# Last projection behind the last gate, running sums begun early, and the right half of the gates as products of split operands

## The reference

```python
h = layer_norm(DEEPNORM_ALPHA * x + mix, ln1_g, ln1_b)
logits = h @ router_w + router_b               # 32 experts, the top 4 for each token
# for each chosen expert e, over the rows sent to it:
gate, up = split(h @ w_gate_up[e] + b_gate_up[e])
y = ((clip(up) + 1) * min(gate, 7) * sigmoid(1.702 * gate)) @ w_down[e] + b_down[e]
ffn = sum over the 4 chosen experts of softmax weight * y
ple = sigmoid(h @ ple_w_gate) * (p @ ple_w_proj)
x = layer_norm(DEEPNORM_ALPHA * h + ffn + ple, ln2_g, ln2_b)
# second block: RMS norm, projections, attention and a recurrence, FFN, RMS norm
```

## Time and profile before

| | |
|---|---|
| median of 3 runs | 2106.93 us (2105.21 to 2108.22) |
| the profiled execution's own time | 2108.97 us |
| its span, first to last instruction | 2107.1 us |
| PE busy | 2073.0 us, 98% of the span |
| DVE, ACT, POOL busy | 1548.6, 1136.7, 237.1 us |
| granted clock of TensorE, mean | 0.993 |

### The profile page before, as it was taken

One profiled execution on the slowest core, in us unless ns is written; L12 is line 12 of the kernel. 1 busy time (PEld: TensorE's weight loads), 2 busy tenths in 40 slices (PEclk: granted clock), 3 DMA queues, 4 the chain that ended last, 5 costly groups with the idle time before them and its releaser, 6 DMA issues.

```text
span 2107.1 us, 26298 instructions
## 1 busy us (share of the span) xinstructions
PE 2073.0 (98%) x9292; PEld 1629.9 (77%) x9292; DVE 1548.6 (73%) x1431; ACT 1136.7 (54%) x1054; POOL 237.1 (11%) x239
## 2 busy tenths in 40 slices
PE   8999999999999999999999999989999999999998
PEld 4864478888888888888888888868886678888887
DVE  6986289999999999999999999974773344333333
ACT  3132177777777777777777777753124523122222
POOL 0006211111111111111111111100000000000000
PEclk9999999999999999999999999999999999999999
DMA  5233499999999999999999999932221213222321
GB/s 223 90 140 124 176 361 383 379 387 377 384 378 384 380 382 379 384 378 386 377 384 378 386 378 384 365 134 80 71 90 61 80 40 110 93 89 98 120 80 40
DMA packets 79062, 522.31 MB, mean 248 GB/s; under 512 B 10352, under 2 KB 10880, under 8 KB 22048
## 3 DMA queue, kind: packets, MB, share of 16 engines
q1 hardware_dynamic: 66496, 483.88, 59.1%
q0 software_dynamic: 9056, 30.62, 5.7%
q10 hardware_dynamic: 3456, 7.06, 1.0%
HBM read 500.92 MB, written 18.60 MB: 247 GB/s over the span
## 4 chain that ended last, share of the span: by engine, by line
PE 94%; DVE 4%; ACT 1%; issue 1%; DMA 0%; DVEq 0%; SPq 0%; ACTq 0%
PE bank L1088 26%; PE bank L1090 26%; PE bank L1089 26%; PE bank L1080 5%; PE bank L1268 1%; PE bank L1406 1%; PE bank L1097 1%; PE bank L1466 1%; PE bank L1225 1%; PE bank L1485 1%; PE bank L1260 1%; PE bank L1126 1%; PE bank L1501 1%; PE bank L1475 1%; DMA ring<-in_wd 0%
## 5 line engine op out<-in xcount | busy, mean ns | idle before, releaser
L1808 DVE TENSOR_TENSOR ring_r<-ring,room_r 128x2048 fp32r<-128x2048 f32 x384 | 875.2, 2294 | 78.6 <-ACT room_r L745 72.6
L745 ACT ACTIVATE room_r<-ring 128x2048 fp32r<-128x2048 f32 x384 | 736.2, 1918 | 175.0 <-PE bank L1090 168.2
L1089 PE MATMUL bank<-ring_r,room_r 128*128 128x512 f32 x1744 | 680.3, 390 | 0.0
L1088 PE MATMUL bank<-room_r 128*128 128x512 f32 x1576 | 624.1, 396 | 3.6 <-DVE room_r L1851 1.9
L1090 PE MATMUL bank<-room_r 128*128 128x512 f32 x1568 | 612.8, 391 | 0.0
L1089 PEld LDWEIGHTS bank<-ring_r,room_r 128*128 128x128 f32 x1744 | 328.5, 188 | 67.3 <-issue 1.7
L1088 PEld LDWEIGHTS bank<-room_r 128*128 128x128 f32 x1576 | 296.9, 188 | 65.7 <-DVE ring_r L1808 4.2
L1090 PEld LDWEIGHTS bank<-room_r 128*128 128x128 f32 x1568 | 295.1, 188 | 62.9
L1088 PE MATMUL bank<-room_r,ring_r 128*128 128x512 f32 x520 | 203.5, 391 | 1.7 <-DVE room_r L2154 0.9
L1090 PE MATMUL bank<-room_r,ring_r 128*128 128x512 f32 x512 | 199.3, 389 | 0.0
L1089 PE MATMUL bank<-ring_r 128*128 128x512 f32 x384 | 149.5, 389 | 0.0
(11 more groups left out here) (289 smaller groups left out, 2137.4 us busy)
## 6 DMA issues: line engine op xcount, KB each, us to landing
ring<-in_wmoe SPq DMA_DIRECT2D x384, 1024.0 KB, 12.0
ring<-in_wf SPq DMA_DIRECT2D x33, 1024.0 KB, 4.8
ring<-in_wd SPq DMA_DIRECT2D x7, 2048.0 KB, 9.4
ring<-in_wp SPq DMA_DIRECT2D x14, 1024.0 KB, 4.9
ring<-in_wo SPq DMA_DIRECT2D x2, 2048.0 KB, 8.5
ring<-in_wd SPq DMA_DIRECT2D x2, 1024.0 KB, 8.9
room<-in_xtok ACTq DMA_DIRECT2D x1, 2048.0 KB, 12.9
h_rows<-room POOLq DMA_DIRECT2D x4, 512.0 KB, 3.0
```

Of the source, the lines that this page charges most:

```text
L745: act.activation(w_hi[s_ % PAIRS], raw_w[ORDER[s_]], ACT.Copy)\
L1088: pe.matmul(out, x_hi, w_hi, start=start, stop=False, skip_group_check=True)
L1089: pe.matmul(out, x_hi, w_lo, start=False, stop=False, skip_group_check=True)
L1808: dve.tensor_tensor(w_lo[i], raw_w[i], w_hi[s_ % PAIRS].bitcast(F32), ALU.subtract)\
```

## The change

1. The groups are numbered anew: g = 0 to 3 are the left half (n = 0) of token tiles 0 to 3, g = 4 to 7 the right half.
2. The four gates of the right half become products of split operands: ACT rounds `hT` (two instructions) and the weights `pg_raw` (one of 128 x 4096), DVE subtracts (three more), and `ple_gate(4)` waits for the last of these. The split operands lie in the places of pieces 1, 2, 3, 4, 5, 7, 8 and 9 of the first block.
3. SP issues the first block's loads in the order `FIRST_LOADS`: piece 0 as before, 10 and 11 behind the fourth gate, then 1, 2, 3, 4, 5, 7, 8 and 9 behind the last gate, and 6 at the end, behind the last projection.
4. `ple_proj(7)` runs behind `ple_gate(7)`; `bias_down(6)` moves to bank 3; PE's waits for the last parts and biases move from before the first block to before `biases(1)` in it.
5. `sum_begun(0)` stands before `rest_of_down`, `sum_begun(i)` before `sum_ended(i - 1)`; DVE makes `token_sel` between its two `half_lo`.

```diff
+FIRST_LOADS = [0, 10, 11, 1, 2, 3, 4, 5, 7, 8, 9, 6]
...
+        hT_hi = ring_at(2 * CH, KT * S, ring_r).rearrange("p (k t) -> p k t", k=KT)
+        hT_lo = [ring_at(at + k * S, S, ring_r) for at in (HW, 3 * CH + HW) for k in range(KT // 2)]
+        pg_raw = slot(4)
+        pg_hi = ring_at(CH, CH, ring_r)
+        pg_lo = ring_at(4 * CH, CH, ring_r)
...
+        def bdn_bank(g):
+
+            return bank[3] if g == 6 else bank[5 * (g % 2)]
...
-                for i in range(PIECES):
+                for i in FIRST_LOADS if first else range(PIECES):
                     if not first:
                         sp.wait_ge(s["used"], after(b, PLACE[i]) if i >= 10 else after(b - 1, PLACE[i]))
+                    elif i == 10:
+                        sp.wait_ge(s["pleg_ready"], TT)
+                    elif i == 1:
+                        sp.wait_ge(s["pleg_ready"], 2 * TT)
                     elif i == 6:
                         sp.wait_ge(s["plep_ready"], 2 * TT)
-                    elif i == 8:
-                        sp.wait_ge(s["pleg_ready"], 2 * TT)
                     sp.dma_start(raw_w[i], a["wmoe"][bass.ts(expert, 1), i].rearrange("o p n -> (o p) n"))\
                       .then_inc(raw_in[i], 16)
 
...
+
+            act.wait_ge(s["hT_done_v"], KT // 2)
+            act.wait_ge(s["hT_done_a"], KT // 2)
+            for q in range(2):
+                part = slice(4 * q, 4 * q + 4)
+                act.activation(hT_hi[:, part, :], hT[:, part, :], ACT.Copy).then_inc(s["zhi_done"], 1)
+            chunk(act, 8)
+            act.activation(pg_hi, pg_raw, ACT.Copy).then_inc(s["zhi_done"], 1)
...
-                i, n = divmod(g, 2)
...
-                i, n = divmod(g, 2)
-                w = chunk(pe, 7 + n).rearrange("p (k c) -> p k c", k=KT)
-                accumulate(bank[1 + g % 2][:, :], [(hT[:, k, i * P:(i + 1) * P], w[:, k, :]) for k in range(KT)])\
-                    .then_inc(s["pleg_ready"], 1)
+                n, i = divmod(g, TT)
+                at = slice(i * P, (i + 1) * P)
+                if g == 2 * TT - 1:
+                    pe.wait_ge(s["ple_parts"], g - 1)
+                if n == 0:
+                    w = chunk(pe, 7).rearrange("p (k c) -> p k c", k=KT)
+                    accumulate(bank[1 + g % 2][:, :], [(hT[:, k, at], w[:, k, :]) for k in range(KT)])\
+                        .then_inc(s["pleg_ready"], 1)
+                    return
+                hi, lo = (w.rearrange("p (k c) -> p k c", k=KT) for w in (pg_hi, pg_lo))
+                pe.wait_ge(s["zlo_done"], 18)
+                for k in range(KT):
+                    ins = product(bank[1 + g % 2][:, :], hT_hi[:, k, at], hT_lo[k][:, at], hi[:, k, :], lo[:, k, :],
+                                  k == 0, k == KT - 1)
+                ins.then_inc(s["pleg_ready"], 1)
...
-                accumulate(bank[5 * (g % 2)][:, :], [(GT[0:E, i * P:(i + 1) * P], bdn[0:E, n * 512:(n + 1) * 512])])\
+                if g == 6:
+                    pe.wait_ge(s["ple_parts"], 2 * TT - 1)
+                accumulate(bdn_bank(g)[:, :], [(GT[0:E, i * P:(i + 1) * P], bdn[0:E, n * 512:(n + 1) * 512])])\
...
             for g in range(4, 2 * TT):
-                ple(g)
+                if g < 2 * TT - 1:
+                    ple(g)
+                else:
+                    ple_gate(g)
+                    ple_proj(g)
                 if g == 2 * TT - 2:
                     gathered(0)
                 bias_down(2 * g - 8)
@@ -1248,8 +1285,7 @@
...
-            pe.wait_ge(s["ple_parts"], 2 * TT)
-            pe.wait_ge(s["bdn_done"], 2 * TT)
+            pe.wait_ge(s["ple_parts"], 2 * TT - 1)
...
                 gate_up(b, 4)
                 gate_up(b, 5)
+                if first:
+                    pe.wait_ge(s["ple_parts"], 2 * TT)
+                    pe.wait_ge(s["bdn_done"], 2 * TT)
                 biases(1)
...
+            def sum_begun(i):
+
+                pe.wait_ge(sum_in[i], 16)
+                for n in range(2):
+                    pe.matmul(bank[2 * i + n][:, :], ident, acc[:, i, n * 512:(n + 1) * 512], start=True, stop=False,
+                              skip_group_check=True)
+
+            def sum_ended(i):
+
+                for n in range(2):
+                    ins = pe.matmul(bank[2 * i + n][:, :], token_sel[0:CAP, i * P:(i + 1) * P],
+                                    y_sb[0:CAP, n * 512:(n + 1) * 512], start=False, stop=True, skip_group_check=True)
+                ins.then_inc(s["sums_ready"], 1)
+
             def token_sums(b):
 
-                for g in range(2 * TT):
-                    i, n = divmod(g, 2)
-                    if n == 0:
-                        pe.wait_ge(sum_in[i], 16)
-                    if g == 0:
-                        pe.wait_ge(s["row_sel_ready"], 1)
-                    part = slice(n * 512, (n + 1) * 512)
-                    pe.matmul(bank[g][:, :], ident, acc[:, i, part], start=True, stop=False, skip_group_check=True)
-                    if n == 1:
-                        if i == 0:
-                            pe.wait_ge(s["y_copied"], b * 2)
-                        for m in range(2):
-                            ins = pe.matmul(bank[2 * i + m][:, :], token_sel[0:CAP, i * P:(i + 1) * P],
-                                            y_sb[0:CAP, m * 512:(m + 1) * 512], start=False, stop=True, skip_group_check=True)
-                        ins.then_inc(s["sums_ready"], 1)
+                sum_begun(1)
+                pe.wait_ge(s["row_sel_ready"], 1)
+                pe.wait_ge(s["y_copied"], b * 2)
+                sum_ended(0)
+                for i in range(2, TT):
+                    sum_begun(i)
+                    sum_ended(i - 1)
+                sum_ended(TT - 1)
...
+                        sum_begun(0)
                         rest_of_down(T, True)
                         token_sums(T)
...
+            for q in range(2):
+                part = slice(4 * q, 4 * q + 4)
+                dve.wait_ge(s["zhi_done"], 16 + q)
+                dve.tensor_tensor(ring_at((0, 3 * CH)[q] + HW, HW, ring_r).rearrange("p (k t) -> p k t", k=KT // 2), hT[:, part, :], hT_hi[:, part, :].bitcast(F32), ALU.subtract)\
+                   .then_inc(s["zlo_done"], 1)
+            dve.wait_ge(s["zhi_done"], 18)
+            dve.tensor_tensor(pg_lo, pg_raw, pg_hi.bitcast(F32), ALU.subtract).then_inc(s["zlo_done"], 1)
             dve.wait_ge(s["bias_hi"], 1)
             dve.tensor_tensor(bias_tab[E:2 * E, :], braw[E:2 * E, :], bias_tab[E:2 * E, :].bitcast(F32), ALU.subtract)\
                .then_inc(s["bias_split"], 1)
...
-                i, n = divmod(g, 2)
+                n, i = divmod(g, TT)
...
-                dve.tensor_tensor(part, part, bank[5 * (g % 2)][:, :], ALU.add).then_inc(s["bdn_done"], 1)
+                dve.tensor_tensor(part, part, bdn_bank(g)[:, :], ALU.add).then_inc(s["bdn_done"], 1)
...
-
-            dve.wait_ge(s["late_in"], 48)
-            dve.wait_ge(s["idx_kept"], T * 2)
-            step(dve.tensor_copy(token_of[0:CAP, :], idx_row[0:CAP, :]))
-            dve.tensor_scalar(token_sel[0:CAP, :], token_row[0:CAP, :], token_of[0:CAP, :], None, ALU.is_equal)\
-               .then_inc(s["row_sel_ready"], 1)
...
             half_lo(0)
+            dve.wait_ge(s["late_in"], 48)
+            dve.wait_ge(s["idx_kept"], T * 2)
+            step(dve.tensor_copy(token_of[0:CAP, :], idx_row[0:CAP, :]))
+            dve.tensor_scalar(token_sel[0:CAP, :], token_row[0:CAP, :], token_of[0:CAP, :], None, ALU.is_equal)\
+               .then_inc(s["row_sel_ready"], 1)
             half_lo(1)
             combine(0)
```

## The result

The changed kernel takes 2110.74 us (median of 15 runs, 2108.23 to 2111.93), the kernel before 2106.88 beside it (15 runs, 2104.80 to 2108.22). The ratio is 1.0018 with a 95% interval of 1.0012 to 1.0025: +3.9 us (2.5 to 5.3), which lies inside the 0.2%, 4.2 us, that I counted as no change. The interval leaves out zero, though: it is a small loss, not nothing. The profiled execution took 2110.09 us, with a span of 2108.2 and a mean granted clock of 0.994.

What follows compares the result with a forecast made beforehand. PE was taken to bound the kernel, busy 98% of the span. -7.6 at the last gate, turned into +1.3 at `turn(0)` by late piece 6, +2.0 clock and +0.3 end gave +3.6 on 2106.93: 2110.5 us, range 2104 to 2114.

Steps and rivals of the forecast that it cites:

- Products, 1.47 a gate: Right half's four gates: 24 fast matmuls instead of 16 plain float32 records save 1.47 us a gate, 5.9 for four.
- The splitting costs nothing: Before `ple_gate(4)`: PE's plain groups hide ACT's roundings and DVE's subtractions; cost 0, up to 9 us without that cover.
- Block 0 entered with no wait: From last gate to first block: PE enters 3.8 us after the last gate ends, at 256.6 not 265.17, without waiting.
- The loads: First block's loads behind the last gate: piece 6 lands 28.7 us after that gate's end (27.5 to 30.7).
- Behind piece 6, 6.5: First block, step 8: rounding 1.9, subtraction 2.3, activations 2.0 and hand-overs, 6.5 us until `turn(0)` at 288.0, +1.3.
- PE ahead of `turn(0)`: First block: PE ends step 7 near 24 us after the last gate, then idles 11 us before `turn(0)`.
- piece 6 is in time: Rival, first block: loads overlap or step 8 isn't held, `turn(0)` at 277.0, -9.7, no slow clock, 2097 us; chance 0.06.
- The clock, 2.0 (1.5 to 2.5): First block, step 8: half-pace clock behind PE's idle time before `turn(0)` loses 2.0 us (1.5 to 2.5).
- Later blocks 0: Blocks after the first: next loads come about 7 us late, but the DMA catches up; cost 0.
- The end, +0.3: End of last block: early sums gain nothing; slow clock in PE's wait for `token_sel`, up to 1.5, taken as +0.3.
- The loads are slow: Rival, first block: loads at 2.9 us a piece, piece 6 2.0 us later, 2112.5; chance 0.37, including upper-end clock or `token_sel` losses.
- Blocks bound by the DMA: Rival, all blocks: three pieces instead of eight under way before the last gate, +5 that stays, 2112 us; chance 0.04.

Runs made afterwards that it cites:

- e2: The changed kernel with the right half's four gates plain float32 again, on rounded weights, splitting and load order kept; 2115.83 us, ratio 1.0038 to the kernel before.
- e4: The kernel before with part 4 alone (last projection behind the last gate, waits moved into the first block); 2102.48 us, ratio 0.9978.
- e1: The changed kernel with piece 6 loaded in its turn, ahead of 7, 8 and 9; 2101.49 us, ratio 0.9973 to the kernel before.
- e8: The changed kernel with 30 fast matmuls, results unread, added between step 7 and `turn(0)` of the first block; 2107.31 us, ratio 1.0002 to the kernel before.
- e3: The kernel before with part 5 alone (early running sums, `token_sel` between the two `half_lo`); 2106.89 us, ratio 1.0001.
- e5: The changed kernel without part 5 (no early running sums, `token_sel` ahead of both `half_lo`); 2109.82 us, ratio 1.0014 to the kernel before.
- e7: The changed kernel with some low parts of `hT` moved to free room, piece 1 loaded early beside piece 0, 6 in its turn; 2097.99 us, ratio 0.9958.
- e6: The changed kernel with ACT's and DVE's activations of chunk 0 ahead of the splitting of step 8; 2106.32 us, ratio 0.9997 to the kernel before.
- e9: The changed kernel with the edits of e7 and e6 together; 2099.93 us, ratio 0.9966 to the kernel before.

## Why the prediction was right

The forecast was 2110.5, +3.6; measured 2110.74, +3.9, and it was so by the mechanism that the prediction named: piece 6 gives the gain back. That the two numbers lie so close is partly luck, as the steps show:

- *Products, 1.47 a gate:* 1.40 (e2's trace); 5.6 for four in place of 5.9. The projection's four records 1.81 in place of 1.7. Together 7.4 for 7.6.
- *The splitting costs nothing:* right. DVE ended the last subtraction at 211.1 (predicted 212.0), and the first product gate began at 218.1 with no wait.
- *Block 0 entered with no wait:* right, at Tg + 3.7 for 3.8. e4 showed something that the prediction had not priced by itself: this alone, with no other part, is worth 4.9 us.
- *The loads:* piece 6 at Tg + 29.5 for 28.7, inside 27.5 to 30.7, but past the Tg + 29.3 from which I had called it slower. From the first landing, where ACT takes piece 1 at 256.91, to piece 6 at 280.33 it was 23.4, just as summed (28.7 - 5.3). What came late is piece 1: Tg + 6.05 for 5.3. The windows from 255 to 270 show 395, 403 and 349 GB/s while the DMA share was 1.0, in sum (25 + 17 + 71) x 5 us = 0.57 MB behind 420, 1.3 us; I had put 1.2 above the lower end of 27.5. It is there that the gather's rows and `sum_rows` run between the pieces, as in the section "Issuing engines are not separate DMA queues" of the Trainium skill's "DMA: Bandwidth & Descriptors". Its figure of about 358 GB/s ("Where 436 GB/s comes from") isn't what the windows behind show: 412 to 426 from 270 on. That the late piece is the cause, and not just a companion, is shown by e1.
- *Behind piece 6, 6.5:* 286.56 - 280.33 = 6.2. `turn(0)` thus at Tg + 35.7 for 35.2.
- *PE ahead of `turn(0)`:* mis-sized, and hidden. I had step 7 ending near Tg + 24 and PE idle for 11 us. It ended at Tg + 28.3, and PE was idle for 7.37, because step 1 waited 3.21 (2.6 summed) with 3.4 us of slow clock behind it, and step 5 another 1.64; the clock behind the early wait stands nowhere in the sum. In after this costs nothing, since piece 6 comes later still. In e1 it shows, `turn(0)` at Tg + 28.8 and 2101.5, so that the 2097 of the rival "piece 6 is in time" was some 4 us too low.
- *The clock, 2.0 (1.5 to 2.5):* mis-sized. 2.8 by the trace, and e8, which takes only this away, gives back 3.4 by the medians. I had scaled from a wait of 2.85; this one was 7.37. `turn(0)` and the 12 matmuls behind it ran slow.
- *Later blocks 0:* right; ACT waited for no DMA after block 0.
- *The end, +0.3:* -0.2 by the pair; e3 and e5 show no difference. PE's new wait was 1.26, for some 1.7, and the clock stayed at 1.00 behind it.
- *Behind `combine(0)`:* not in the sum. -1.25 by the traces, cause open.

Made again with these numbers from the start of group 2: -7.4 + 9.3 (`turn(0)`: 86.9 us in place of 84.96, +1.9) + 2.8 - 0.2 - 1.25 = +3.2, and the medians say 3.9 +/- 1.4. So `turn(0)` and the clock came out 0.6 and 0.8 dearer than summed, and 1.8 us at and behind the end made up for it. Of the rivals, "piece 6 is in time" was excluded by the wait of 8.05. "The loads are slow" didn't come true as a pace: the landing was 0.8 of its 2.0 late, and by piece 1. "Blocks bound by the DMA" was excluded by the list of waits.

What is not settled: where the 1.25 us behind `combine(0)` come from; whether e7's waits of 4.0 us are the same in every execution (its interval is 2.8 to either side); and how much of them could be taken away by other places for the split operands, or by another buffer for ACT's first steps. Neither was tried, and the product gates were never run without part 4.

## What to carry to other kernels

Where a buffer is borrowed for a faster computation, the price is the time at which it comes free, and it is paid by the transfers that were to use it: count from the release, in the order of the queue, to the first piece that is needed, and sort the queue by when each piece is needed, not by which place is free first. e1 is the whole difference between a change that loses 3.9 us and one that brings 5.9. But the cheap part should be run by itself too: e4, which borrows nothing, brings 4.9. A wait of PE costs itself and, in these traces often, a stretch of slow clock behind it, so that one long wait is dearer than its length. Taking away waits of 2.85 and 1.65 (e4, 4.9 us) was worth about as much as making the four gates ahead of them faster (5.6).

## What the runs showed of the hardware that I had not expected

- The slow stretch behind a wait of PE in these traces: behind 7.37 us (after), from 286.6 to 292.4 at 1.2 GHz; behind 5.61 (e6), from 286.8 to 290.3; behind 3.21 (after), from 261.6 to 265.0; behind 2.90 (e1), from 262.3 to 268.4; behind 1.94 at the end of the blocks (before), from 1389.5 to 1392.8. Behind waits of 0.59 to 0.79 (e4, e7, e9) the clock stayed at 1.00, and behind 1.26 (after) and 1.31 (e1), 1.64 (after) and 1.65 (before) too. Behind 1.21 (e9, with one of 0.38 just after) the matmuls from 291.9 to 295.2 were slow. And behind 2.39 (e2) it stayed at 1.00. So in these runs the length of the wait alone doesn't say whether the clock falls.
- The same stretch of plain matmuls at 190 to 195 got a clock of 0.66 or of 1.00 from one profiled execution to the next (0.66 in before, 1.00 in e3, with the same code up to there), 1.7 us, almost half of what was to be measured here. Two profiles alone would have given +1.1 for a change of +3.9.
